# Two runs of unread TensorE products taken out of the router's tail

## What is computed

```python
pg = softmax(xt @ w_rg + b_rg)               # 4 groups
g_w, g_idx = top_k(pg, 1)
le = (xt @ w_re + b_re).reshape(n_tok, 4, 8) # 32 experts, 8 in a group
tv, tj = top_k(le[group of the token], 2)
w_top = softmax(tv) * g_w                    # two experts for each token
# each expert, on the tokens sent to it:
gu = xb @ w_e1[e]                            # 1024 -> 2 * 512
y  = (silu(gu[:, :512]) * gu[:, 512:]) @ w_e2[e]
```

## Time and profile before

| | |
|---|---|
| median of 3 runs | 1674.19 us (1673.24 to 1674.54) |
| profiled execution, its own time | 1668.83 us |
| its span, first to last instruction | 1667.0 us |
| TensorE busy | 1324.9 us, 79% |
| VectorE busy | 587.1 us, 35% |
| ScalarE busy | 448.4 us, 27% |
| mean granted TensorE clock | 0.909 of full |
| moved by DMA | 534.19 MB, mean 320 GB/s |

### The profile page before, as it was taken

One profiled execution on the slowest core, in us unless ns is written; L12 is line 12 of the kernel. 1 busy time (PEld: TensorE's weight loads), 2 busy tenths in 40 slices (PEclk: granted clock), 3 DMA queues, 4 the chain that ended last, 5 costly groups with the idle time before them and its releaser, 6 DMA issues.

```text
span 1667.0 us, 30744 instructions
## 1 busy us (share of the span) xinstructions
PE 1324.9 (79%) x13385; PEld 1020.6 (61%) x13385; DVE 587.1 (35%) x916; ACT 448.4 (27%) x648; POOL 0.4 (0%) x5
## 2 busy tenths in 40 slices
PE   6999999998677675767677999998987655666665
PEld 5999999985354352535347999997944323433332
DVE  6658746544121201102016785565421100110102
ACT  6454444532120111011014445445310000101001
POOL 0000000000000000000000000000000000000000
PEclk8999999999889798988867999998999987987886
DMA  9843458349999999999997326672699999999993
GB/s 346 297 167 115 152 179 334 131 155 392 417 426 422 427 427 423 426 423 427 427 390 262 122 94 211 247 260 101 239 384 428 427 427 427 426 427 425 427 428 157
DMA packets 94021, 534.19 MB, mean 320 GB/s; under 512 B 10018, under 2 KB 14522, under 8 KB 67900
## 3 DMA queue, kind: packets, MB, share of 16 engines
q1 hardware_dynamic: 90900, 522.24, 78.0%
q10 hardware_dynamic: 2984, 9.91, 1.5%
HBM read 525.84 MB, written 6.29 MB: 319 GB/s over the span
## 4 chain that ended last, share of the span: by engine, by line
PE 51%; DMA 39%; DVE 6%; issue 2%; ACT 2%; SPq 0%; DVEq 0%; ACTq 0%
DMA ring<-in_w_expert_out 32%; PE banks L1541 28%; DMA ring<-in_w_expert_in 6%; PE banks L1568 6%; PE banks L1918 5%; PE banks L1874 4%; PE banks L1929 2%; PE banks L1891 1%; DVE stat L1402 1%; PE banks L1738 1%; DVE w_lo L954 1%; PE banks L1754 1%; PE banks L1676 0%; DVE arena L1397 0%; DVE xT L1097 0%
## 5 line engine op out<-in xcount | busy, mean ns | idle before, releaser
L1874 PE MATMUL banks<-ring,arena 128*32 128x256 f32 x3968 | 286.1, 439 | 152.0 <-DMA ring<-in_w_expert_in 145.4
L1874 PEld LDWEIGHTS banks<-ring,arena 128*32 128x32 f32 x3968 | 133.6, 123 | 284.9 <-DMA ring<-in_w_expert_in 179.2
L954 DVE TENSOR_TENSOR w_lo<-ring,w_hi 128x2048 fp32r<-128x2048 f32 (+1 forms) x105 | 215.1, 2049 | 133.9 <-ACTq L575 122.0
L1541 PE MATMUL banks<-h_hi,w_hi 128*128 128x256 f32 x784 | 223.3, 285 | 0.1
L1541 PE MATMUL banks<-h_hi,w_lo 128*128 128x256 f32 x784 | 221.8, 283 | 0.0
L1395 DVE TENSOR_TENSOR arena<-arena,banks 128x128 f32<-128x128 f32 x65 | 18.8, 289 | 564.7 <-ACT arena L909 564.7
L1918 PE MATMUL banks<-ring,arena 128*32 128x256 f32 x2016 | 147.7, 442 | 79.7 <-DMA ring<-in_w_expert_out 67.6
L909 ACT ACTIVATE arena<-banks 128x128 f32<-128x128 f32 x65 | 18.1, 278 | 697.1 <-PE banks L1874 697.1
L1541 PE MATMUL banks<-h_lo,w_hi 128*128 128x256 f32 x720 | 203.7, 283 | 0.0
L598 ACT CAST w_hi<-ring 128x2048 fp32r<-128x2048 f32 (+1 forms) x105 | 179.9, 1714 | 82.8 <-PE banks L1541 34.2
L1918 PEld LDWEIGHTS banks<-ring,arena 128*32 128x32 f32 x2016 | 72.5, 124 | 136.3 <-issue 49.7
(11 more groups left out here) (346 smaller groups left out, 2101.4 us busy)
## 6 DMA issues: line engine op xcount, KB each, us to landing
ring<-in_w_expert_in SPq DMA_DIRECT2D x124, 2048.0 KB, 23.7
ring<-in_w_expert_out SPq DMA_DIRECT2D x63, 2048.0 KB, 24.7
ring<-in_w_in SPq DMA_DIRECT2D x24, 2048.0 KB, 8.9
ring<-in_w_branch SPq DMA_DIRECT2D x12, 1024.0 KB, 5.0
ring<-in_w_out SPq DMA_DIRECT2D x4, 2048.0 KB, 7.9
ring<-in_w_xq SPq DMA_DIRECT2D x4, 2048.0 KB, 10.7
spare_unit<-in_w_expert_in SPq DMA_DIRECT2D x4, 2048.0 KB, 12.8
ring<-in_w_xo SPq DMA_DIRECT2D x4, 2048.0 KB, 7.9
```

What stands on the lines that cost most here:

```text
L954: post(dve.tensor_tensor(piece_view(w_lo, *key), piece_view(ring, *key), high_view(*key).bitcast(F32), ALU.subtract), "w_split")
L1541: ins = pe.matmul(acc, stationary(a, k), moving(b, k), start=k == 0 and n == 0, stop=k == kc - 1 and n == 2)
L1874: ins = pe.matmul(G[32 * j:32 * j + 32, :], xTe[:, k, e * SL:(e + 1) * SL], w[:, k % 4, :, j * P:(j + 1) * P], start=k == 0, stop=k == KC - 1,
```

## The change

Both calls of `stay_warm` and the helper go. The waits for banks 0 and 1, the wait for the mask and all else stay where they are.

```diff
-                def stay_warm(n):
-
-                    for _ in range(n):
-                        pe.matmul(psum[:, 1, 0:T], ident, iota[:, 0:T], start=True, stop=True)
-
                 pe.wait_ge(bank_free[0], JOB[layer, "moe", 0][2])
                 pe.wait_ge(bank_free[1], JOB[layer, "moe", 1][2])
-                stay_warm(14)
                 pe.wait_ge(S["mask_ready"], layer + 1)
                 acc = job_begin(pe, layer, "place")
                 pe.matmul(acc[:, 0:NE], tri, mask[:, 0, :], start=True, stop=True)
...
                 acc = job_begin(pe, layer, "count")[:, T:]
                 pe.matmul(acc[0:NE, 64:65], mask[:, 0, :], ones[:, 0:1], start=True, stop=False)
                 done(pe.matmul(acc[0:NE, 64:65], mask[:, 1, :], ones[:, 0:1], start=False, stop=True))
-                stay_warm(3)
```

## The result

The changed kernel takes 1675.70 us (median of 20 runs, 1672.91 to 1680.63). The kernel before takes 1669.26 us (median of 20 runs, 1666.83 to 1674.54), not 1674.19, the median of the first three of these 20. The ratio is 1.0031 (95% interval 1.0021 to 1.0040): slower by 5.2 us (3.5 to 6.7); the two medians differ by 6.4 us.

What follows compares the result with a forecast made beforehand. The expert weight stream, restarted late after the router, was taken as the bound: 0.55 us place delay plus 2.3 us at half clock, twice, gave 5.7 us on 1674.19, so 1679.9 us, range 1676.4 to 1683.2.

Steps and rivals of the forecast that it cites:

- What bounds the kernel: Expert stages: one DMA weight stream without slack; TensorE's first release after the router, if late, delays its end equally.
- The direct saving of 0: Router tail: removing the 14 and the 3 products frees 0 us of the path, to 0.2 us for both layers.
- The clock ahead of the gather: Router tail, both layers: some 7 us of TensorE idling drops the clock to 0.50 from about 380 to 389 us.
- The place delay: Place products behind the mask, at 1.2 GHz: the gather starts 0.55 us later per layer, bounds 0 and 0.89.
- The gather and first products at half clock: After the router: a cold stretch of 4.4 to 5.9 us loses 2.3 us per layer, bounds 1.5 and 3.5.
- The sum per layer: First weight release of the experts: late by 0.55 + 2.3 = 2.85 us in each of two layers, 5.7 us together.
- the base: Whole kernel: starting level 1674.19 us, the median of the runs, 5.36 us above the profiled execution, carried over.
- That the clock stays up: Rival, router tail: the clock stays full or the lateness is absorbed, about 1674.2 us; chance 0.10.
- 3.9 us of idling at 1.00: Evidence for the full-clock rival: from 435.6 us, 3.9 us without a TensorE record left the clock at 1.00.
- That it stays down much longer: Rival, gather and first products: some 15 us at half clock, loss 14.3 us, time 1688.5 us; chance 0.03.
- The products stood in nobody's way: Rival, TensorE's queue ahead of place: the products delay it, so removal gains; chance 0.04 of over 0.2% faster.

Runs made afterwards that it cites:

- Experiment 2: Kernel before with 22 unread products in place of 14 ahead of the mask, all else as before: 1675.39 us, ratio 1.0033.
- experiment 3: Two kernels against the kernel before: only the last 3 products kept, 1678.57 us, ratio 1.0047; only the first 14 kept, 1673.70 us, ratio 1.0019.
- Experiments 6 and 7: Six unread products put into the cross-attention waits: in the kernel before 1666.47 us, ratio 0.9986; in the changed kernel 1674.30 us, 1.0024 against the kernel before.
- experiment 4: Kernel before with 7 unread products in place of 14 ahead of the mask, the last 3 kept: 1675.53 us, ratio 1.0031.
- experiment 1: Kernel before with all 17 unread products kept in place but 2 columns wide instead of 256: 1675.15 us, ratio 1.0027.

## Why the prediction was right on the change and wrong on the time

**What bounds the kernel: right.** The stream of weights starts late and ends late. Experiment 2 shows it with no clock involved.

**The direct saving of 0: right as far as it shows.** For the last 3 it is shown: without them, layer 1 of experiment 3 stayed at full clock and kept its 16.34 us. For the 14 it rests on the trace of before, since no layer without them stayed at full clock. Products held the gather up only where they ran at half clock (experiment 3) or where eight more reached past the mask (experiment 2).

**The clock ahead of the gather: right.** It was down at the gather in all six layers seen of the changed kernel. In layer 0 of the first profile it fell shortly before 380 us, where I had said 380, and rose at 393 against 389; the DMA pause ended 6 us later, against 2 to 4. I had counted both without the 3.1 us that came from ahead of the router.

**The place delay, 0.55 us: it measured 0.61**, 1.50 against 0.89. The Trainium skill (TensorE: Matmul & The Clock Gate, LDWEIGHTS), whose load time has no term for the clock, would have it at about 0.1, by an estimate from that figure; the trace disagrees again. A further 0.19 us I had not: "place" starts 8.21 us behind the router group instead of 8.02, with the mask no later. The gather thus starts 0.80 us late.

**The gather and first products at half clock, 2.3 us: they measured 1.97 and 1.90**, from the gather's start to the first load: 7.44 and 7.37 us against 5.47. The 4.7 us of half clock behind 388.29 lie between the two stretches I had taken it from, 4.4 and 5.9, and near the lower.

**The sum per layer, 2.85 us: 2.77 and 2.69 in this profile**, 2.3 to 2.8 in all. Twice that against a measured 5.2 (3.5 to 6.7).

**The step that failed is the base**: "The median of the runs is 5.36 us higher, which the trace doesn't explain; I carry the difference over". The three runs, 1673.24 to 1674.54, lay at the top of what 20 runs show. The profiled execution, 1668.83, was near their median of 1669.26. On that base the same sum gives 1669.26 + 5.7 = 1675.0, against 1675.70. That the profile lay near the median was luck: the profiled execution of the changed kernel was the longest of its 20. What lifted the first three runs isn't shown, since none of them was profiled. The trace did hold a sign: the earlier trace rows argue from a clock that falls or stays with the moment, and the same trace shows L1754 at 3.72 us in one layer and 6.49 in the other. I had that pair in reach and didn't draw from it that two executions of one kernel can differ by 3 us a layer. Experiments 6 and 7 show that this place is a part of the spread. The range had no term for the base at all; the observed spread of 7.7 us in the kernel before is wider than the range.

**The rivals.** That the clock stays up needed a shorter gap: with some 3.75 us, small records in it, it stayed up in one layer of two. What I had for it, 3.9 us of idling at 1.00, was the first part of 6.82 us in which the clock did fall (experiment 4). That it stays down much longer didn't happen. The kind of work does matter: with three 2-column products ahead of it the gather and what follows ran 5.1 and 4.3 us at half clock in the two layers (experiment 1), with three of 256 columns 0.8 and 0.4 us (experiment 3). The products stood in nobody's way.

## What to carry to other kernels

Before taking out work whose result nobody reads, look at the clock rows on both sides of it and at what the next real product releases: here 17 unread products that cost nothing hold a start of the weight stream that is worth 2.3 to 2.8 us a layer. A short gap may cost in one execution and not in the next, as those of 3.7 to 3.9 us did here, so look for the same group of records at two durations, and fill the gap where its successor is on the path. When you read an idle stretch, take it up to the record that ends it. And give the range a term for the base: neither three runs nor one profile is a level. Here three runs that agreed within 1.3 us were all some 4 to 5 us above the median of 20.

## What the runs showed of the hardware that was not expected

TensorE's clock fell to half 2.1 us into a run of records of 2 columns in which the profile shows it busy without a break (experiment 1), and it fell around gaps of 0.6 or 0.9, 1.1 and 1.0 us with short transposes between (L1754 in the cross-attention, at half clock in 13 of the 16 layers profiled without the filling; the three at full clock are all layer 0). Its busy time in the profile was thus no sign here that the clock would hold. The Trainium skill (TensorE: Matmul & The Clock Gate, What's actually happening) says that the number of slow products of one kernel differs from run to run; the trace agrees, with 3.72 us for the 16 records of L1754 in layer 0 of one profile of the changed kernel and 6.59 us in the other.

After 7.24 us of idling "place" started 0.19 us later behind its mask than in the kernel before, which had idled for 0.92 us; with the narrow products, 3.01 us idle and also at half clock, it did not, nor with seven products and 3.93 us. It is 8.20 to 8.23 us behind the router group in all eight layers with 7.2 us of idling and 8.01 or 8.02 in the others with a wait for the mask. I don't know the cause.
